# Zeros by GpSimd, the bonus sum one step later, and head readouts of six steps on the HGRN banks, in the recurrent stage of a two-block kernel

## The reference

```python
p = layer_norm(x) * (1 + scale) + shift ; p = p @ w_in        # tokens and a context of 256 tokens
pool, u, fh, g = split(p)                                     # 256, 3*384+4*64, 4*384, 1024 columns
# RWKV, 6 heads of 64, two directions, state S (64x64) per head:
S = S * w_t - (S kk_t) (kk_t * a_t)^T + v_t k_t^T ;  y_t = S r_t
y = group_norm(y) * gn_g + gn_b + sum(r * k_mod * r_k) * v    # the last sum is the "bonus"
# HGRN, 6 heads of 64, two directions, chunks of 32, gates f_t:
S = f_t * S + k_t i_t^T ;  o_t = q_t S
o = o / sqrt(mean(o*o) + eps) * norm_g                        # per head
x = layer_norm(ALPHA * x + gate * ((concat(pool, y, o) * silu(g)) @ w_out)) * ln_g + ln_b
```

## Time and profile before

| | us |
|---|---|
| median of 3 runs | 1725.4 (1723.82 to 1725.76) |
| the profiled execution | 1722.1 |
| its span, first to last instruction | 1720.2 |
| TensorE busy | 1625.2 (94%) |
| VectorE busy | 467.8 (27%) |
| ScalarE busy | 336.2 (20%) |
| GpSimd busy | 13.1 (1%) |
| mean granted TensorE clock | 0.975 |

### The profile page before, as it was taken

How to read it: one execution, slowest core, us unless ns; L and a number is a source line. 1 busy time by engine, 2 the same in 40 slices (tenths; PEclk the granted TensorE clock), 3 DMA queues, 4 the chain that set the end, 5 groups by cost and what they waited for, 6 DMA issues and landing times.

```text
span 1720.2 us, 25915 instructions
## 1 busy us (share of the span) xinstructions
PE 1625.2 (94%) x11539; PEld 1285.4 (75%) x11539; DVE 467.8 (27%) x1047; ACT 336.2 (20%) x704; POOL 13.1 (1%) x29
## 2 busy tenths in 40 slices
PE   6999966989799999999999999999999999999998
PEld 1445455878688778767788888888777778888887
DVE  1331034564653232314421200001322333210001
ACT  1200052343532311124310000000103340000000
POOL 2000000000000000000000000000000000000000
PEclk9999987989899999999999999999999999999999
DMA  9422200000002423442244444444442333344440
GB/s 366 160 98 74 86 13 1 3 2 4 17 3 100 122 86 113 147 147 98 98 147 147 147 147 147 147 147 124 147 147 98 115 130 125 128 159 159 161 159 28
DMA packets 110862, 191.27 MB, mean 111 GB/s; under 512 B 20872, under 2 KB 27280, under 8 KB 110624
## 3 DMA queue, kind: packets, MB, share of 16 engines
q1 hardware_dynamic: 109216, 186.20, 31.3%
q10 hardware_dynamic: 576, 2.11, 0.3%
q0 software_dynamic: 960, 1.33, 0.2%
HBM read 188.57 MB, written 1.05 MB: 110 GB/s over the span
## 4 chain that ended last, share of the span: by engine, by line
PE 90%; ACT 3%; DVE 3%; DMA 1%; issue 1%; DVEq 1%; ACTq 1%; SPq 1%
PE psum L1052 28%; PE psum L1196 13%; PE psum L1137 9%; PE psum L1275 8%; PE psum L781 5%; PE psum L1060 4%; PE psum L706 3%; PE psum L1220 2%; PE psum L1296 2%; PE psum L1251 2%; PE psum L938 2%; PE psum L1123 1%; DMA arena<-in_mod_w 1%; PE psum L1166 1%; PE psum L697 1%
## 5 line engine op out<-in xcount | busy, mean ns | idle before, releaser
L1052 PE MATMUL psum<-arena 128*128 128x256 f32 x2208 | 480.6, 379 | 0.0
L1052 PEld LDWEIGHTS psum<-arena 128*128 128x128 f32 x2208 | 417.6, 189 | 61.5 <-issue 1.3
L1651 ACT ACTIVATE arena<-psum 128x512 f32<-128x512 f32 (+6 forms) x230 | 119.7, 527 | 612.0 <-PE psum L1052 132.6
L1196 PE MATMUL psum<-arena 128*128 128x256 f32 x1024 | 222.2, 378 | 0.0
L1196 PEld LDWEIGHTS psum<-arena 128*128 128x128 f32 x1024 | 193.7, 189 | 28.2
L1137 PE MATMUL psum<-arena 128*128 128x256 f32 x768 | 176.5, 382 | 0.0
L1137 PEld LDWEIGHTS psum<-arena 128*128 128x128 f32 x768 | 141.8, 189 | 26.5 <-issue 5.3
L1275 PE MATMUL psum<-arena 128*128 128x512 f32 (+1 forms) x368 | 140.1, 538 | 2.1 <-issue 1.4
L1275 PEld LDWEIGHTS psum<-arena 128*128 128x128 f32 x368 | 68.7, 189 | 72.7 <-issue 68.0
L781 PE MATMUL psum<-arena 64*64 64x64 f32 x3072 | 98.0, 220 | 0.8 <-issue 0.8
L781 PEld LDWEIGHTS psum<-arena 64*64 64x64 f32 x3072 | 93.9, 136 | 6.2 <-issue 4.1
(11 more groups left out here) (315 smaller groups left out, 1284.2 us busy)
## 6 DMA issues: line engine op xcount, KB each, us to landing
arena<-in_w_in SPq DMA_DIRECT2D x33, 2048.0 KB, 7.7
arena<-in_w_up SPq DMA_DIRECT2D x16, 2048.0 KB, 7.6
arena<-in_w_down SPq DMA_DIRECT2D x16, 2048.0 KB, 7.9
arena<-in_mod_w SPq DMA_DIRECT2D x6, 2048.0 KB, 13.0
arena<-in_w_out SPq DMA_DIRECT2D x6, 2048.0 KB, 8.0
arena<-in_w_branch SPq DMA_DIRECT2D x6, 2048.0 KB, 8.0
arena<-in_w_in SPq DMA_DIRECT2D x3, 1024.0 KB, 7.4
arena<-in_w_in SPq DMA_DIRECT2D x12, 256.0 KB, 4.7
```

The source lines that it names most:

```text
L1052: mm = pe.matmul(b[:, i * T:(i + 1) * T], w[:, k, c:c + P], src[:, k, :], start=k == 0, stop=k == ks - 1)
L1196: mm = pe.matmul(bs[t][:, 0:T], w[:, k, t * P:(t + 1) * P], hff[:, c * KT + k, :], start=c == 0 and k == 0, stop=c == 3 and k == KT - 1)
L1651: return act.activation(dst, src, ACT.Copy, scale=scale)
```

## The change

The zeros go to GpSimd, which waits for the same count of used buffers; ScalarE waits for them ahead of its first S step in turn 0, and VectorE where it wrote them. E gets a tenth step: the bonus product and VectorE's use of it come one step later. Q and N get six steps instead of four, with their instructions at other steps. N of turns 0 and 1 uses the HGRN pool's banks instead of the prepare pool's (Y stays in the prepare pool). The order of the list changes: behind E, in the second half of I, and in the chain, where H starts one C step earlier and ends ahead of the last one. In the last turn the I steps stand between the Q and N steps, one M stands ahead of the chain instead of three, and seven stand behind Y instead of five.

```diff
-TAIL = "TETETEETEEHEHTEHEHTHTH"
+TAIL = "TETETEETEEHEHTEHEHTHETH"
         if more:
             n = "N" if j else ""
-            turns += list(f"IEQ{n}IEIEQ{n}IEIEQ{n}EQ{n}IE" + "CECECHCHCHCHCHCH" + "Y")
+            turns += list(f"IEQ{n}IEQ{n}IEQ{n}IEIEQ{n}EQ{n}IEQ{n}" + "CECHCHECHCHECHCHC" + "Y")
         else:
-            turns += list("IQNIQNIQNQN" + "IMIMIM" + "CMCMCMCMCMCMCMCM" + "Y" + "MNMNMNMMN")
+            turns += list("IQNIQNIQNQNIQNIQNIM" + "CMCMCMCMCMCMCMCM" + "YMNNMNMNNMMMMN")
-    "E": [..., [], [], [], [], [], [("bonus", "D", 1)], []],
+    "E": [..., [], [], [], [], [], [], [("bonus", "D", 1)], []],
-    "Q": [[], [("osq", "A", 1)], [], []],
-    "N": [[("yc", "D", 1)], [("yvar", "A", 1)], [], []],
+    "Q": [[], [], [("osq", "A", 1)], [], [], []],
+    "N": [[("yc", "D", 1)], [], [("yvar", "A", 1)], [], [], []],
 def pool_of(x, j, k):
-    if x in "YN":
-        return "rwkv" if j == JT - 1 else "prepare"
+    if x in "YN" and j == JT - 1:
+        return "rwkv"
-    return {"T": "tail", "E": "prepare", "Q": "hgrn", ...
+    return {"T": "tail", "E": "prepare", "Y": "prepare", "N": "hgrn", "Q": "hgrn", ...
 # GpSimd
+            if first:
+                gp.wait_ge(s_used, 15)
+                for x in (lkm, akb, xf, acc):
+                    gp.memset(x, 0.0)
+                gp.drain().then_inc(sem("zeroed"), 1)
 # TensorE: prepare_tensor
-            for _ in range(5):
+            for _ in range(6):
                 yield
             pe.wait_ge(sem("e_bonus"), j + 1)
 # TensorE: rwkv_out_tensor
-            pool = y_pool(j)
-            pool.wait_emptied(pe, f"y_{j}")
+            of, pool = y_pool(j), norm_pool(j)       # norm_pool: rwkv in the last turn, else hgrn
+            of.wait_emptied(pe, f"y_{j}")
             pe.matmul(take_bank(pool, f"yc_{j}")[:, 0:T], cst("centre"), yacc[:, j, :], ...)
+            yield
             yield
             b = take_bank(pool, f"yvar_{j}")
 # ScalarE: score_scalar
+            if j == 0:
+                act.wait_ge(sem("zeroed"), 1)
 # ScalarE: rwkv_out_scalar: Square in step 1 (was 0), Ln in 3 (was 2), Exp in 4 (was 3)
 # ScalarE: hgrn_out_scalar: Square in step 0, Ln in 3 (was 2), Exp in 4 (was 3)
 # VectorE: prepare_vector: one more step ahead of the bonus
 # VectorE: score_vector
             if j == 0:
-                dve.wait_ge(s_used, 15)
-                dve.memset(xf, 0.0)
-                dve.memset(lkm, 0.0)
-                dve.memset(akb, 0.0)
-                dve.memset(acc, 0.0)
+                dve.wait_ge(sem("zeroed"), 1)
 # VectorE: rwkv_out_vector: first pair in step 2 (was 0), second in step 5 (was 3)
+            yield
+            yield
             pool.wait_filled(dve, f"yc_{j}")
 # VectorE: hgrn_out_vector: last multiplication in step 5 (was 3)
```

More of the change, by code:

```diff
@@ L247, in order_of_streams @@
             n = "N" if j else ""
-            turns += list(f"IEQ{n}IEIEQ{n}IEIEQ{n}EQ{n}IE" + "CECECHCHCHCHCHCH" + "Y")
+            turns += list(f"IEQ{n}IEQ{n}IEQ{n}IEIEQ{n}EQ{n}IEQ{n}" + "CECHCHECHCHECHCHC" + "Y")
         else:
-            turns += list("IQNIQNIQNQN" + "IMIMIM" + "CMCMCMCMCMCMCMCM" + "Y" + "MNMNMNMMN")
+            turns += list("IQNIQNIQNIQNQNIQNIM" + "CMCMCMCMCMCMCMCM" + "YMNNMNMNNMMMMN")
     met = collections.Counter()
@@ L289, in pool_of @@
 def pool_of(x, j, k):
-    if x in "YN":
-        return "rwkv" if j == JT - 1 else "prepare"
+    if x in "YN" and j == JT - 1:
+        return "rwkv"
     if x == "S":
         return "rwkv" if k else "prepare"
-    return {"T": "tail", "E": "prepare", "Q": "hgrn", "H": "hgrn", "M": "out"}.get(x, "rwkv")
+    return {"T": "tail", "E": "prepare", "Y": "prepare", "N": "hgrn", "Q": "hgrn", "H": "hgrn", "M": "out"}.get(x, "rwkv")
 def plan_of(pool):
@@ L1032, in y_pool, with norm_pool @@
             return rw if j == JT - 1 else ep
+        def norm_pool(j):
+            return rw if j == JT - 1 else hg
         def turns_of(stream, *args):
@@ L1566, in rwkv_out_scalar @@
         def rwkv_out_scalar(act, j, copy, done, emptied):
-            pool = y_pool(j)
+            pool = norm_pool(j)
+            yield
             pool.wait_filled(act, f"yc_{j}")
@@ L1999, in rwkv_out_vector @@
         def rwkv_out_vector(dve, j, done, emptied, bc, fence):
-            pool, m = y_pool(j), mix[:, 2 + j, :]
+            pool, m = norm_pool(j), mix[:, 2 + j, :]
+            yield
+            yield
             pool.wait_filled(dve, f"yc_{j}")
@@ L2024, in hgrn_out_vector @@
             dve.scalar_tensor_tensor(m, oacc[:, j, :], col("hgrn_norm_g", j), m, ALU.mult, ALU.mult)
-            yield
-            yield
-            yield
+            for _ in range(5):
+                yield
             dve.wait_ge(sem("o_scales"), j + 1)
```

## The result

| | before | after |
|---|---|---|
| median, us | 1724.7 (1723.8 to 1725.8) | 1706.9 (1706.0 to 1710.3) |
| the profiled execution | 1722.1 | 1706.3 |
| its span | 1720.2 | 1704.5 |
| mean granted TensorE clock | 0.975 | 0.979 |

The ratio is 0.9907, 95% interval 0.9894 to 0.9921. The change is faster by about 0.9%: 17.8 us in the medians and 15.7 in the spans. The two differ because the profiled execution of before, 1722.1, was faster than all four of its timed ones. Spans of one kernel scatter too: the four timed ones of after have spans of 1704.2 to 1708.5 us.

The account below looks back on a forecast made before the run. In the recurrent stage, waits of one in-order engine for another were taken to set the time. 3.3 - 0.3 + 1.8 + 4.2 = 9.0 us gained, from the median 1725.4 to 1716.4 us, range 1711 to 1724.

Parts of the forecast that it names:

- part 2: Chain of turns 0 and 1, bonus sum and stream H moved: 0.3 us lost in turn 0, 0.4 gained in turn 1.
- part 1: Turn 0, the zeros written by GpSimd instead of VectorE: 3.3 us gained at 7.1 us of zeroing.
- part 3: Head readouts of turn 1: yc 2.5 us earlier, but yvar then waits for its bank, so 1.4 us gained.
- Part 4: Head readouts of turn 2: a 2.63 us wait and 1.53 us of low clock go, 4.2 us gained.
- A: Rival on the zeros: GpSimd at half VectorE's rate or a 7 us drain, 1723.5 us; 15 in 100.
- C: Rival on ScalarE's wait for the zeros: zeroing at three times VectorE's time makes it slower, 1730.6 us; 5 in 100.
- D: Rival on the readouts: yc and yvar block each other and ScalarE's later Exp holds i6, 1722.1 us; 5 in 100.
- I take off 0.8: Turn 0, zeros: 0.8 us off the 4.1 gained at t0, for TensorE work at the lower clock.
- Sum of turn 0: 0.3 us lost: Chain of turn 0: bonus product +1.0, H's wait -1.1, Y's wait +0.2, up to 0.5 for low clock.
- the 0.4 that I had added for a late copy and the clock: Chain of turn 0: up to 0.2 us for Y waiting on ScalarE's last copy, up to 0.5 for low-clock work.
- Rival B: TensorE's clock in turns 0, 1 and the S stage: full clock returns later, 4.5 us less gain, 1720.9 us; 13 in 100.
- No part of the change is there, so that part can only move as a block: From 620 to 1700 us, TensorE busy 1073.1 of 1080 us at full clock: no change of its own expected.

Follow-up runs that it names:

- the first experiment: The kernel before with only the zeros moved to GpSimd and the two waits on them: 1718.2 us, ratio 0.9965.
- 15 products: The changed kernel with 15 dummy products, never read, between the first two chain products in turns 0 and 1: 1708.2 us, ratio 0.991.
- late waits: The changed kernel without ScalarE's wait for the zeros, and VectorE's moved to the first masked copy into lkm: 1705.1 us, ratio 0.9888.
- early pair: The changed kernel with VectorE's first two readout multiplications one step earlier, ahead of its decay step E2: 1706.9 us, ratio 0.9901.

## Why the prediction was wrong in size

The spans moved by 6.7 us more than predicted. By the stretches, part 2 has about 3.8 of them, part 1 1.8, part 3 0.4 and the rest of the kernel 1.1, less 0.5 that the start took.

**Right.** Part 4: 4.2 predicted, 4.20 measured, with the first output group at 2.00 us and clock 1.00. Wait and low clock went as worked out, but the exact hit is partly luck: TensorE now waits 1.45 us ahead of an inverse step at 522.48, where it was 0.49 at the same place before, and smaller savings elsewhere in the turn made up for that. Part 3: yvar became late at about the predicted size, a wait of 1.17 us; t0 to C0 of turn 1 gained 1.8 where 1.4 was worked out; 0.5 of that came with the zeros alone. Rivals A, C and D fall: the zeroing took 6.2 us, not 14 or 21, the drain showed no 7 us here, and the readouts blocked nothing more.

**Part 1, mis-sized.** 3.3 predicted, 5.1 measured by the first experiment. 0.9 is the zeroing, 6.18 us instead of 7.1. The step "I take off 0.8" for the clock was about right up to t0: the low stretch, 288.3 to 291.7 us, held the transposes and part of up0, which took about 1.0 us longer than worked out (3.5 us from ScalarE's first copy to up0 instead of 2.6), so gate to t0 gained 3.9. What the prediction put at nothing is the time behind t0. Before, the low stretch lasted to 301.3 us, 2.6 us past t0; after, full clock was back before t0. That gave the other 1.2 us.

**Part 2, the step that failed.** "Sum of turn 0: 0.3 us lost" and 0.4 gained in turn 1, against 1.2 and 2.7 gained. The bonus product was right (0.9 measured, 1.0 predicted). The place of H was right in turn 0 as a number, 1.1, but by luck: I had named the 1.14 us wait, which is gone, and at full clock the place is worth only 0.4. In turn 1 it was worth 3.6 instead of 1.8. I had read TensorE's own waits, 1.14 us ahead of the H product, and not VectorE's wait for TensorE of 2.52 and 3.73 us, which says that TensorE set the time up to the second chunk's state, at half clock. With H0 ahead of the second chunk's right sides, its transposes run while VectorE is busy anyway. VectorE's scans of H then fill what was its wait, and the low stretch is over or hidden when it comes to wait. The experiments show the parts: 0.4 us per turn from the order at full clock, 0.7 and 3.2 more at the clock that is granted. In turn 0 the two edits together account for 0.3 of the 1.2 us; 0.6 came with the zeros alone, whose low stretch ends at 16.1 instead of 17.8 us behind C0. The 0.3 left, and the 0.4 that I had added for a late copy and the clock, no run isolates.

**Rival B, the clock, had the wrong sign.** It let each new gap cost 1.5 us. In the stretch itself the low clock did stay, at 0.79 and 0.80; its cost went, but for 0.3 us in turn 0 (32.5 with 15 products instead of 32.8).

**The rest of the kernel.** "No part of the change is there, so that part can only move as a block": layer to end took 1.1 us less. It was not all at full clock, as the prediction had it: early in it, before has stretches at 1.2 GHz of 6.8 us at 605.1 and at 649.5, after of 3.4 at 588.6 and 6.8 at 633.0. Over all kernels here it was 1113.3 to 1117.7 us, with no relation to the edit that I could show, but with one to the clock: in those without dummy products at its start it was 1113.3 at clock 0.94 in the first 56.8 us, 1115.9 twice at 0.91 and 1116.6 to 1117.7 in the rest, at 0.86 to 0.88. The dummy products at its start gave 0.94 as well, yet 1117.5 and 1115.9; what sets it stays open. It puts a noise of 1 to 2 us on each span, as does the start, 280.8 to 283.0. It also hid most of the gains of the late waits, the early pair and the bonus product when each was tried alone.

## What to carry to other kernels

Where two in-order engines hand work to each other, read the wait on each side: the side that waits names the other as the bound, and a product's place is worth what it takes out of that interval, at the clock granted there. Here the idle gap of TensorE behind C0 was followed by work at 1.2 GHz wherever products didn't fill it wholly; put there what the other engine doesn't wait for, and don't count the low stretch itself as a loss. Measure an edit from a landmark ahead of all it moves: C1 to Y looked 3.8 us better and nothing was gained.

## What the hardware showed

- GpSimd wrote 7168 columns of 128 partitions in 6.18 us, 0.86 ns per column. VectorE's four take 6.2 us themselves (1.76 for 2048 columns, 0.91 for 1024) and 7.1 with the gaps between them, so here the two engines fill equally fast. The Trainium skill, GPSIMD Engine Reference, section Performance versus the Vector engine, has GpSimd at about half VectorE's rate, measured on an add of two inputs; for this fill, which has no input, the trace does not agree. By the same section a body of one or two operations is bound by its ports at 1.03 cycles per element. At the 1.2 GHz of that page's table this is 0.86 ns, an estimate from the page's figures, and with that the trace agrees.
- The drain behind these memsets and the wake-up took 0.34 us together; the one behind the 20 DMA issues at the start again came with a gap of 7.0 us.
- Filling 6.6 us of an idle gap of 7.0 and 7.8 us with products didn't remove the stretch at 1.2 GHz: it came 12 and 9 us later, at 358 instead of 346 us and at 450 instead of 442, and was shorter, 3.4 and 6.8 us instead of 13.7. Of the runs here only those whose products left no gap at all had clock 1.00 from C0 to Y.
